# An expert's gate and up loads queued ahead of the previous expert's down load, in halves with semaphores of their own

## The reference

```python
    y = jnp.zeros_like(hf)
    for e in range(N_EXPERTS):                                   # 16 experts
        u = jax.nn.silu(jnp.dot(hf, w_e_gate[e])) * jnp.dot(hf, w_e_up[e])   # 1024 -> 512
        y = y + gates[:, e:e + 1] * jnp.dot(u, w_e_down[e])                  # 512 -> 1024
```

## Time and profile before

| what | value |
|---|---|
| median of 3 runs | 1476.72 us (1476.27 to 1479.73) |
| the profiled execution | 1478.23 us, its span 1476.5 us |
| expert stage in the span | from about 932 us to the end |
| lists | 27, on 16 experts |
| transitions | 15: after lists 1, 3, 6, 9, 10, 12, 14, 15, 17, 18, 19, 21, 23, 24 and 25, for experts 1 to 15 in turn |
| PE busy in the span | 1276.9 us (86%) |
| DMA traffic | 215.01 MB, mean 146 GB/s |
| gate, up and down loads | 16 each, 2048 KB each, median 11.0, 15.8 and 15.2 us from issue to landing |

### The profile page before, as it was taken

The page is one execution under the profiler, slowest core; times in us unless marked ns, Lnnn a source line. Parts: engine busy times, 40 slices in busy tenths (PEclk is TensorE's granted clock), DMA queues, the critical chain, the costliest instruction groups (busy, mean ns, idle before and its releaser), DMA issues. The chain is left out here.

```text
span 1476.5 us, 21409 instructions
## 1 busy us (share of the span) xinstructions
PE 1276.9 (86%) x6661; PEld 919.6 (62%) x6662; DVE 771.5 (52%) x1187; ACT 545.0 (37%) x916; POOL 264.5 (18%) x287
## 2 busy tenths in 40 slices
PE   5529999999999999994969973699999999969964
PEld 0014666665766666564648863588888787858853
DVE  0010656466475655647244446555528665865752
ACT  0011535435253443524143330444416444644540
POOL 1000101102010110204000000233133233323313
PEclk7759999999999999995779995799999999989988
DMA  9970000000000000005273328458667979898874
GB/s 355 415 286 11 5 15 0 14 0 14 14 0 14 0 14 0 14 2 130 38 202 124 118 100 291 151 182 273 215 184 250 332 256 309 300 309 253 266 281 85
DMA packets 87921, 215.01 MB, mean 146 GB/s; under 512 B 16577, under 2 KB 20289, under 8 KB 84818
## 3 DMA queue, kind: packets, MB, share of 16 engines
q1 hardware_dynamic: 75794, 170.58, 32.3%
q0 software_dynamic: 12096, 44.05, 11.4%
HBM read 188.31 MB, written 26.23 MB: 145 GB/s over the span
## 5 line engine op out<-in xcount | busy, mean ns | idle before, releaser
L481 PE MATMUL psum<-w_in_sb,x_res 128*128 128x512 f32 (+1 forms) x864 | 353.2, 563 | 4.4 <-DVE x_res L471 4.4
L481 PEld LDWEIGHTS psum<-w_in_sb,x_res 128*128 128x128 f32 x864 | 160.9, 191 | 164.1 <-issue 156.8
L1942 PE MATMUL psum<-e_w_h,e_x_h 128*128 128x512 f32 x432 | 174.9, 405 | 29.5 <-DVE w_gu L2055 23.1
L1943 PE MATMUL psum<-w_gu,e_x_h 128*128 x432 | 171.8, 398 | 0.0
L1944 PE MATMUL psum<-e_w_h,e_x_l 128*128 128x512 f32 x432 | 171.6, 397 | 0.0
L2055 DVE TENSOR_TENSOR w_gu<-w_gu,e_w_h 128x1024 f32 x128 | 146.7, 1220 | 20.5 <-ACT e_w_h L1996 20.5
L1996 ACT ACTIVATE e_w_h<-w_gu 128x1024 fp32r x128 | 123.0, 1048 | 53.9 <-issue 33.0
L1889 POOL DMA_INDIRECT out<-e_work,e_to x26 | 87.6, 3371 | 302.3 <-DVE e_work L2043 302.3
L1942 PEld LDWEIGHTS psum<-e_w_h,e_x_h 128*128 128x128 f32 x432 | 83.4, 193 | 47.9 <-DVE w_gu L2055 23.6
L1944 PEld LDWEIGHTS psum<-e_w_h,e_x_l 128*128 128x128 f32 x432 | 83.3, 193 | 18.2
L1943 PEld LDWEIGHTS psum<-w_gu,e_x_h 128*128 128x128 f32 x432 | 83.4, 193 | 17.0
(11 more groups left out here) (393 smaller groups left out, 2055.9 us busy)
## 6 DMA issues: line engine op xcount, KB each, us to landing
w_gu<-in_w_e_gate SPq DMA_DIRECT2D x16, 2048.0 KB, 11.0
w_gu<-in_w_e_up SPq DMA_DIRECT2D x16, 2048.0 KB, 15.8
w_dn<-in_w_e_down SPq DMA_DIRECT2D x16, 2048.0 KB, 15.2
stage<-in_w_ada SPq DMA_DIRECT2D x24, 1024.0 KB, 13.2
x_res<-in_x SPq DMA_DIRECT2D x20, 512.0 KB, 3.7
w_in_sb<-in_w_in SPq DMA_DIRECT2D x5, 2048.0 KB, 19.0
out<-r_x SPq DMA_DIRECT2D x9, 512.0 KB, 2.6
h_d<-r_h SPq DMA_DIRECT2D x9, 512.0 KB, 2.9
```

What stands on the lines that cost most here:

```text
L481: last = pe.matmul(psum[:, PJ0 + j % 2, 0:n], h_t[:, k, :], b["w_in_sb"][:, k, a:a + n], start=(k == 0), stop=(k == KC - 1))
L1942: pe.matmul(psum[:, j, :], x_h[:, k, :], wh, start=(k == 0), stop=False)
L1943: pe.matmul(psum[:, j, :], x_h[:, k, :], wl, start=False, stop=False)
```

## The change

The loads of one expert are no longer one function. `load_gate_up` issues four DMAs of 1 MB instead of two of 2 MB (first the half k = 0 to 3 of gate and of up, then k = 4 to 7) and counts each half on a semaphore of its own. `load_down` is as before. SP's order becomes gate and up of expert e + 1, then down of expert e. Each still waits for the last use of the buffer it overwrites. On ACT the wait for all gate and up weights becomes one wait ahead of k = 0 and one ahead of k = 4.

```diff
-def load_expert(sp, b, d, e, par, after_gu=None, after_dn=None):
-
-    if after_gu:
-        sp.wait_ge(*after_gu)
-    for j, w in enumerate((d["w_gate"], d["w_up"])):
-        sp.dma_start(b["w_gu"][:, par, j, :, :], w[one(e), :, :].rearrange("a (k p) n -> p (a k) n", p=P)).then_inc(b["gu_loaded"][par], 16)
-    if after_dn:
-        sp.wait_ge(*after_dn)
+def load_gate_up(sp, b, d, e, par):
+
+    for half in range(2):
+        ks = slice(half * (KC // 2), (half + 1) * (KC // 2))
+        for j, w in enumerate((d["w_gate"], d["w_up"])):
+            sp.dma_start(b["w_gu"][:, par, j, ks, :],
+                         w[one(e), half * (D // 2):(half + 1) * (D // 2), :].rearrange("a (k p) n -> p (a k) n", p=P)
+                         ).then_inc(b["gu_loaded"][half][par], 16)
+
+
+def load_down(sp, b, d, e, par):
+
     sp.dma_start(b["w_dn"][:, par, :, :], d["w_down"][one(e), :, :].rearrange("a (k p) n -> p (a k) n", p=P)).then_inc(b["dn_loaded"][par], 16)
...
-            def load(e, par):
-
-                done = sp.value_load(b["list_info"][0:1, bass.ds(e + (SLOTS - 2), 1)], min_val=0, max_val=LISTS)
-                load_expert(sp, b, d, e, par, (s["gu_mm"], done + 1), (s["dn_mm"], done + 1))
-
-            with sp.Fori(1, NE // 2) as i:
-                load(i * 2, 0)
-                load(i * 2 + 1, 1)
+            def uses_done(e):
+
+                return sp.value_load(b["list_info"][0:1, after(SLOTS - 2, e)], min_val=0, max_val=LISTS)
+
+            def gate_up(e, par):
+                sp.wait_ge(s["gu_mm"], uses_done(e) + 1)
+                load_gate_up(sp, b, d, e, par)
+
+            def down(e, par):
+                sp.wait_ge(s["dn_mm"], uses_done(e) + 1)
+                load_down(sp, b, d, e, par)
+
+            gate_up(2, 0)
+            with sp.Fori(1, NE // 2 - 1) as i:
+                gate_up(i * 2 + 1, 1)
+                down(i * 2, 0)
+                gate_up(i * 2 + 2, 0)
+                down(i * 2 + 1, 1)
+            gate_up(NE - 1, 1)
+            down(NE - 2, 0)
+            down(NE - 1, 1)
...
-            def weights_in(e):
-                act.wait_ge(gu_loaded[0], (e // 2 + 1) * 32)
-                act.wait_ge(gu_loaded[1], (e + 1) // 2 * 32 + 1)
-
             def split_gu(e, ks):
                 for k in ks:
+                    if k % (KC // 2) == 0:
+                        act.wait_ge(gu_loaded[k // (KC // 2)][0], (e // 2 + 1) * 32)
+                        act.wait_ge(gu_loaded[k // (KC // 2)][1], (e + 1) // 2 * 32 + 1)
```

More of the change, by code:

```diff
@@ L324, in stream_layer @@
             w_gu=sb(top, "w_gu", [P, 2, 2, KC, DE]), w_dn=sb(top, "w_dn", [P, 2, DE // P, D]),
-            gu_loaded=[sem("gu_loaded0"), sem("gu_loaded1")], dn_loaded=[sem("dn_loaded0"), sem("dn_loaded1")])
+            gu_loaded=[[sem(f"gu_loaded{half}{par}") for par in range(2)] for half in range(2)], dn_loaded=[sem("dn_loaded0"), sem("dn_loaded1")])
         route(nc, b, d, router_bias)
@@ L1618, in _ @@
             sp.dma_start(bias[:, :], router_bias.partition_broadcast(P)).then_inc(s["bias_loaded"], 16)
-            sp.sem_inc(b["gu_loaded"][1], 1)
+            for half in range(2):
+                sp.sem_inc(b["gu_loaded"][half][1], 1)
             sp.sem_inc(b["dn_loaded"][1], 1)
             for e in range(2):
-                load_expert(sp, b, d, e, e)
+                load_gate_up(sp, b, d, e, e)
+                load_down(sp, b, d, e, e)
         @block.gpsimd
@@ L1834, in _ @@
         def _(sp):
-            def load(e, par):
-                done = sp.value_load(b["list_info"][0:1, bass.ds(e + (SLOTS - 2), 1)], min_val=0, max_val=LISTS)
-                load_expert(sp, b, d, e, par, (s["gu_mm"], done + 1), (s["dn_mm"], done + 1))
-            with sp.Fori(1, NE // 2) as i:
-                load(i * 2, 0)
-                load(i * 2 + 1, 1)
+            def uses_done(e):
[15 more added lines that the diff above has]
+            down(NE - 1, 1)
             for par in range(2):
-                sp.wait_ge(gu_loaded[par], NE * 16 + par)
+                for half in range(2):
+                    sp.wait_ge(gu_loaded[half][par], NE * 16 + par)
                 sp.wait_ge(dn_loaded[par], NE // 2 * 16 + par)
@@ L2014, in _ @@
             e0 = act.value_load(b["list_info"][0:1, 0:1], min_val=0, max_val=NE - 1)
-            weights_in(e0)
             split_gu(e0, range(0, FIRST_PART))
@@ L2028, in step @@
                 with act.If(e > 0):
-                    weights_in(e)
                     split_gu(e, range(KC))
```

## The result

The changed kernel takes **1519.32 us** (median of 5 runs, 1517.11 to 1521.38), the kernel before 1478.75 us beside it (5 runs, 1476.27 to 1479.73). The ratio is **1.0274**, 95% interval 1.0258 to 1.0291: slower by 40.6 us, where 62 were forecast, and inside the range given.

The account below looks back on a forecast made before the run. Expert stage bound by PE's steps of 17.72 us, with 36.1 us lost to weight waits, slower clock and late silus. Losses of 36.4 + 29.2 + 18.0 + 14.6 = 98.2 replace these: +62.1, 1539 us, range 1500 to 1578.

Parts of the forecast that it names:

- The mechanism: Expert stage: down loads queued behind 4 MB of gate and up come late at all 14 transitions; 1495 to 1580 us, chance 0.87.
- H: Expert stage: start of a transition's silu, which is also the end of the previous expert's last hidden.
- S: Expert stage: start of ACT's `split_dn` in a transition; undisturbed it comes 9.85 us after H.
- The threshold of 14.9: Late down load: PE's next-but-one hidden is delayed by (S - H) - 14.9 us, and by nothing below that.
- The lone landing, H + 22: Transitions after lists 3, 6, 12, 21, none adjoining another: S at H + 22, between 19.0 and 24.2; 9.1 us lost each.
- clock (2.0 a stall): PE after a stall: first matmuls run at the lower clock level, adding 2.0 us, between 1.3 and 2.8.
- The chains: Transitions in successive lists share delay: pairs (9, 10; 14, 15) lose 14.6 us each, triple (17 to 19) 18.0, last (23 to 25) 14.6.
- the cover of 9.2: From `split_dn` to PE's next-but-one hidden: four splits, silu, u, x and its low part take 9.24 us.
- the signs of being wrong: Profile after: down loads landing before H + 18, hidden earlier than S + 9.2, or chains losing as much as lone transitions.
- The halves: Half semaphores let `split_gu` start before the second half lands; gate and up being ahead in the new order, put at nothing.
- Faster: Rival: down loads still arrive in time and all 36.1 us come back, 1441 us; chance 0.06.
- The clock rival: Rival: PE's clock stays low through all of a hidden, adding 11.3 instead of 2.0 us in eight groups, 1613 us; chance 0.05.

Follow-up runs that it names:

- order alone: Against the kernel before, only the load order changed: gate and up stay two DMAs of 2 MB with one semaphore per buffer; 1516.68 us, ratio 1.025.
- down held back, in front: Against the changed kernel, the down load waits for the same hidden but is issued ahead of the next gate and up; 1465.89 us, ratio 0.9905.
- The run with small gathers: Changed kernel without POOL's adding DMA of lists 0 to 25, its two gathers per list cut from 512 KB to 64 KB; 1509.09 us, ratio 1.0208.
- the two runs with less POOL traffic: Changed kernel without POOL's adding DMA: 1515.37 us, ratio 1.0243; the same with gathers also cut to an eighth: 1509.09 us, ratio 1.0208.
- the half-between kernel: Against the changed kernel, half of the next gate and up is issued ahead of the down load, half behind it; 1460.91 us, ratio 0.9876.

## Why the prediction was right, and where its sizes were off

**The mechanism held at the lone transitions.** Down loads are issued 3.2 to 3.5 us after H, behind 4 MB, and land too late at every one of them. A hidden starts 9.1 to 9.3 us after `split_dn` (1094.18 - 1084.89 = 9.29; forecast S + 9.2 from the earlier trace rows). The threshold of 14.9 stood from both sides: S - H = 13.9 lost nothing, 16.35 (down held back, in front, second of a pair) lost 1.3 us. The experiments name the cause: order alone gives the loss, the same moment of issue without the 4 MB in front gives none, and halving the bytes moves the loss with the landing time.

**The forecast was 24.1 us of loss too high (98.2 for 74.1), in two terms.**

*The lone landing, H + 22.* I put it between 19.0 and 24.2. The 22 itself followed from no row: one transfer of a set of three that costs 5.2 would have given 19.0 + 1.7 = 20.7. I went higher because POOL's adding DMA is issued at H + 14.3. Measured are 19.8, 19.9 and 19.8, and 22.2 after list 3. With next to no POOL traffic it was still 19.7 to 20.8. So the down load takes its clear 5.1 us there (up lands at 1066.91 + 12.5 = 1079.4, down at 1084.5), and the adding DMA does not stand in its way. Without that DMA only the one after list 3 came earlier (20.4); why it was late stays open. The four cost 29.5 instead of 36.4: 6.9 of the 24.1. What is left over the delay, which I had called clock (2.0 a stall), is 1.2 to 2.5 us in these four. It is no fixed price: the 1.3 us lost at S - H = 16.35 are no more than the delay alone (1.4), and the first matmul after that stall took 0.50 us, as at the upper level, and not 0.79.

*The chains.* Here the sum had a wrong step and not only wrong sizes. It strung 2 MB pieces after one another, added a full set of POOL transfers (5.2) per transition, and took the loss from the last `split_dn` so found: 45.3 for the second of a pair. It came at 40.6, 41.7 and 41.1. The run with small gathers shows what the sum left out: the next gate and up can't be issued before the next hidden ends, so 37.7 is what the chain takes by itself, not 34.9. POOL's traffic adds 3 to 4 us to that, not 10.4.

Nor does the second landing set what a pair costs. It moved from 40.6 and 41.7 to 38.5 and to about 37.7 in the two runs with less POOL traffic, and the pairs' loss stayed (7.9 and 9.4; 8.0 and 8.8; 8.4 and 8.3). PE in the changed kernel, at the transitions after lists 9 and 10 (first H = 1124.46):

```profile
1154.37 0.80 PE L1961 MATMUL psum<-e_w_h,e_x_h 128*128 128x512 f32 x1 [2.75 <-DVE w_gu L2071]
```

This hidden starts 29.9 after H instead of 24.15, and from here to the end of the pair PE has no gap. So this pair pays for its first transition (5.8 us of delay at this row, and 2.2 over it, which I count as clock), and the second late down load ends under that. In the other pair it is 7.3 and 2.2. The row also shows that the cover of 9.2 is one of lone transitions: in a chain ACT and DVE go on to the next gate and up, PE waits for their split, and such a hidden starts 10.1 to 10.6 after the first `split_dn`. PE's waits for `w_gu`, which were to vanish, are these. The pairs cost 17.3 instead of 29.2, the last chain 9.8 instead of 14.6. Of the signs of being wrong, one was that chains lose as much as lone transitions: a pair as a whole did (7.9 and 9.4 beside 6.0 to 9.8), because its second transition added next to nothing.

That the triple came out right (17.5 for 18.0; its third `split_dn` at 66.3 for 66.4) was luck, for what fills that time is not what the sum added up. Even without most of POOL's traffic it came at 63.3, where the pieces alone give 50.8. The third gate and up wait for the hidden that the first late `split_dn` held up; in the changed kernel they are issued 44.0 after the first H (1335.08), and the third `split_dn` starts 22.2 later, where the lone ones need 19.6 to 22.1 from the same issue.

*The halves.* "Nothing" was right for the changed kernel, since gate and up are never late there. With the order of before they win 0.7%, which the change gives away together with the early down loads.

**The rivals.** Faster fell, because gate, up and down back to back took 1084.5 - 1065.2 = 19.3 us and not 15. The Trainium skill's fit ("DMA: Bandwidth & Descriptors", anatomy of one DMA) gives, by estimate, 16.4 for these bytes; the page made it for one DMA issued from GpSimd, and for these five from SP the trace disagrees. The clock rival fell too. In this stretch, from the late silu of list 4 to that of list 5 (columns as in the earlier trace rows), the granted clock averages 0.73:

```profile
1028.10:1047.40 19.30, 15.06 (x55) 11.94 (x56) 5.65 (x6) 2.11 (x5) 4.14 (x6) 0.73 0.34 82
```

That transition (after list 3) cost 2.5 us beyond its delay, not 11.3.

## What to carry to other kernels

When two loads share one queue, ask for each which one is needed first after the moment at which both are issued, and how many bytes stand ahead of it; whether the engine that waits has slack decides from how many bytes on it costs. Here 0 or 2 MB ahead cost nothing and 4 MB cost 6 to 10 us a time. Splitting gate and up so that their consumer can start on a part won 0.7% where they were late, and it also gave the pieces between which a more urgent load fits; splitting the down load too won nothing that was measured. Where late loads follow one another, their delays don't simply add up: ask which of them the engine that sets the end still waits for, and what the issue of the next load waits for. A wait that grows (30.3 to 70.7 us on ACT) is no loss while the engine that sets the end doesn't wait for what stands behind it.

## What the runs showed of the hardware

One thing I had not expected: how long POOL takes to issue the adding DMA depends on what DVE does meanwhile. From the page after the change (mean ns of one, second number):

```profile
L1908 POOL DMA_INDIRECT out<-e_work,e_to x26 | 50.2, 1932 | 381.6 <-DVE e_work L2059 380.2
```

Before, the mean of the same 26 issues was 3371 ns. Eleven of them took 5.8 us, as the one at 1121.57, the others 1.6; after the change only two are long. DVE's four down splits (`tensor_tensor` with two SBUF inputs) in the kernel before and in the half-between kernel, where the same issue is at 1122.00 and takes 1.61 us:

```profile
1121.23 4.62 DVE L2062 TENSOR_TENSOR w_dn<-w_dn,e_w_dh  x4
...
1122.78 4.63 DVE L2081 TENSOR_TENSOR w_dn<-w_dn,e_w_dh  x4 [1.03 <-ACT e_w_dh L2027]
```

The long issue starts 0.3 us after the first split does and ends at 1127.34, 1.5 us after the last: as if it waited for all four and then took its 1.6. The short one starts ahead of them, and the row gather behind it comes 4.6 us earlier after H. DVE's four splits take no longer there (4.63 us), though the first begins while that issue still runs. The Trainium skill, "SBUF — State Buffer", who interferes with whom, states that a DVE instruction with two SBUF inputs contends with a GpSimd instruction that reads SBUF. The rows are as that says, if issuing this DMA is such a read, which no run shows. The same section infers that such DVE instructions don't hold up the making of a DMA's descriptors; the adding DMA was held up here, so for it the measurement decides.

The other is how little POOL's own transfers (44 MB, a fifth of all traffic) slowed the weight loads beside them. From one row I had taken 2 MB to need 10.5 us instead of 5.3 there; leaving out 38 of the 44 MB won 10.2 us of 1519 in all.
